# Two blocks in one kernel: row sums through DRAM, interleaved first stripes, a norm by token tile, and block 2's rows kept on chip

## The chip, the core and the metric

One core of a Trainium2 chip runs the whole program in one launch. Its engines are TensorE (PE, matmuls and transposes), VectorE (DVE), ScalarE (ACT), GpSimd (POOL) and SyncE (SP, which here only issues DMAs). The metric is the device time of one launch in microseconds. Three runs of the kernel before gave 2902.57, 2904.52 and 2905.27; the median is 2904.52.

## The reference, cut to what matters

Input is one sequence of 256 tokens of width 2048, all in float32. Two blocks follow each other.

```
block 1: shift, scale, gate = split(silu(c) @ w_ada + b_ada);  same for the context
  h  = rmsnorm(x) * (1 + scale) + shift;      p = h @ w_in            (9216 columns)
  hc = the same for 256 context tokens;       kc, vc = hc @ w_in[K, V]
  attention of 12 query heads over [k, kc];   fourier mix of u_b (fft over tokens and channels)
  y = (sig(g_a) * ((attn*silu(z_a)) @ w_proj_a) + sig(g_b) * ((mix*silu(z_b)) @ w_proj_b)) @ w_out
  x = rmsnorm(x + gate * y) * final_g
block 2: six modulation vectors = silu(c_2) @ w_mod + b_mod
  u = rmsnorm(x)*norm1*(1+scale1)+shift1;     proj = u @ w_in_2       (18464 columns)
  o_a = stick-breaking attention, 16 heads (sigmoids times running products)
  q, k, v = silu(causal conv of 4 taps);  g = -exp(a_log)*softplus(a_b + dt_bias);  beta = sig(b_b)
  o_b = gated delta rule, 16 heads:  gc = cumsum(g);  decay[r,i] = exp(gc[r]-gc[i]) for i <= r;
        a triangular system per 64 tokens (here solved per 128), a state carried over
  h = x + gate1 * ((sig(gate_a)*(o_a @ p_a) + sig(gate_b)*(o_b @ p_b)) @ w_out)
  u = rmsnorm(h)*norm2*(1+scale2)+shift2
  h = h + gate2 * ((silu(u @ w_gate) * (u @ w_up)) @ w_down)           (5632 wide)
```

## The kernel before

**Chunks and stripes.** All large products run as one stream. A stripe is 512 output columns for 256 tokens (two token tiles m of 128, one PSUM bank each); a chunk is 256 rows of a stripe's weights, 512 KB, as two 128x512 tiles. To keep float32's precision weights and activations are split in two parts each: ACT writes `w_hi` (L412), DVE writes `w_lo = raw - w_hi` (L422), and PE does x_hi*w_hi, x_lo*w_hi (L666) and x_hi*w_lo (L672), 12 matmuls per chunk. Activations stand transposed in `hT` or `fT`, each as hi and lo.

**Buffers.** SP loads raw chunks into six slots (L362), and there are three slots of split weights. At beat n (one beat per chunk) ACT and DVE split chunk n+3 once PE is done with chunk n; SP loads chunk n+6. Each engine is in order: whatever it waits for holds its next split.

**Modulation.** Eight stripes of block 1's modulation ("ada", 64 chunks) have only two tokens as operand: 4 matmuls per chunk (L652, L656), and one chunk per stripe is taken unsplit (`plain`, L642). ACT copies each row out (L868), PE turns it into columns (L876), and DVE and ACT prepare the first operands from it (L893, L903, L909). The other 28 x 8 modulation chunks are elementwise products with sums on DVE (L686), placed at fixed beats (`mod_at`).

**Order.** `of_chunk` is the order: three ada stripes, then a quarter (2 chunks each) of the first three ordinary stripes (two of the context, one of w_in), two ada stripes, a quarter, three ada stripes, two quarters; then phases in1, ab1 (the two projections, merged by gates), out1, in2 (starts at chunk B), pb2, ab2, out2, ffa (gate and up, starts at FFB), dna (down, first 12 chunks per stripe), ffb, dnb (down, the rest). Everything else is a side track: a list of (beat, steps), where `yield k` puts the following instructions at that beat after the start; a track is itself in order, so a later item waits for the end of an earlier one.

**Ends of stripes.** A "store" stripe is copied from PSUM by ACT and DVE and stored to DRAM. A "rows" stripe (out1, out2, dnb) is multiplied by the gate and added to the rows `E[:, 0:2]` by DVE (`add_rows`, L456, L459, L461, L463), and ACT sums squares (L474, L481). In dna the stripes are stored to DRAM, `h2` too, and `base_dve` (L1049, L1052) brings both back early in dnb.

**Norms.** Between out1 and in2, and between out2 and ffa, no product can run before the row norm. DVE reduces the sums (L488 to L498), POOL takes the power -1/2 (L502), DVE scales (L509), PE transposes (L524), ACT writes hi (L534) and b - hi (L540), DVE writes lo (L548). in2's first chunk waits for lo.

**Small projection and running sums.** `w_ba` (2048x32) is loaded at beat B+12 in pieces of 128 bytes (L1369), split by ACT and DVE (L1401, L1428) and multiplied (L1376, L1377). From its columns come the decays; for each of four turns (4 heads, GD_AT) PE makes gc along rows by 8 matmuls of a broadcast column with an upper triangle (L1574, "R"), read by DVE (L1763, L1767) and ACT from PSUM.

**Block 2's attention** (SB_AT, 8 turns of 2 heads; L1997, L2005, L2012, L2020 on PE) stands in one track with the turns of the delta rule and with the transposes of its output (L940) on PE, ACT and DVE.

**Merge gates.** In ab2 SP loads the gates at beat 3 of the first turn (L744), and ACT takes their sigmoid at its beat 1 (L757), waiting for the load.

Of the kernel before, what the change touches and what calls it, by code (L numbers as in the profile page):

```python
# [20 lines left out]
F32 = mybir.dt.float32  # L21
# [5 lines left out]
P = 128  # L27
D = 2048
# [109 lines left out]
def program(nc, a, y_out, dram):  # L138
    ctx = ExitStack()
    with ctx:  # L140
# [60 lines left out]
        ff_sig, ff_row, mg_tmp = E[:, 0, 0:M * W], E[:, 1, 0:M * W], E[:, 1, M * W:]  # L201
# [82 lines left out]
        for k in range(4):  # L284
            st = stripe("dna", 2 * FA, tile_of(a["w_down_2"], k * W), fT, 0, "store", cols_of(dram.ya, k * W))
# [3 lines left out]
        plan(S)  # L289

# [6 lines left out]
        of_chunk = whole(ADS[:3]) + quarter(0) + whole(ADS[3:5]) + quarter(1) + whole(ADS[5:]) + quarter(2) + quarter(3)  # L297
# [11 lines left out]
        ends = {st.end - 1: st for st in ADS + S}  # L309
        at_chunk = {}  # L310
# [60 lines left out]
        def store(sp, st):  # L371
            if st.kind == "store":
                sp.wait_ge(s["ev_act"], st.sn)
                sp.wait_ge(s["ev_dve"], st.sn)
                sp.dma_start(st.dst, ost[:, st.slot]).then_inc(s[f"stored{st.slot}"], 16)
            elif st.phase == "dnb":
# [65 lines left out]
        def add_rows(dve, st):  # L442

            cols = slice(st.o * W, (st.o + 1) * W)
            if st.o == 0:

                dve.wait_ge(s["gr_ld"], 16 * ((st.res - 1) // 4 + 1))
                if st.phase != "dnb":
# [5 lines left out]
            staging(dve, st)  # L454
            o = ost[:, st.slot]
            nc.vector.tensor_tensor(o, ps[:, st.bank:st.bank + M], bm(E[:, 3, cols], M), ALU.mult).then_inc(s["res_mul"], 1)  # L456
# [5 lines left out]
            else:  # L462
                nc.vector.tensor_tensor(E[:, 0:2, cols], E[:, 0:2, cols], o, ALU.add).then_inc(s["res"], 1)  # L463

        def square_rows(act, st):
# [10 lines left out]
            if st.phase != "dnb":  # L476
# [7 lines left out]
        def norm_stat_dve(dve, u):  # L484

            dve.wait_ge(s["sq"], (16, 24)[u])
            wait(dve, s["n_rs"], 2 * u)
            nc.vector.tensor_reduce(nms[:], nss[:].rearrange("p k m o -> p (k m) o"), AX.X, ALU.add).then_inc(s["n_v"], 1)  # L488
            dve.wait_ge(s["n_v"], 3 * u + 1)
            if u == 0:  # L490
                nc.vector.tensor_scalar(nms[:], nms[:], 1.0 / D, None, ALU.mult).then_inc(s["n_v"], 1)
                dve.wait_ge(s["n_v"], 2)
                nc.vector.tensor_scalar(nms[:, 0:M], nms[:, 0:M], EPS, None, ALU.add).then_inc(s["n_v"], 1)
                dve.wait_ge(s["n_v"], 3)
                nc.vector.scalar_tensor_tensor(nms[:, M:], nms[:, 0:M], EPS, nms[:, M:], ALU.mult, ALU.add).then_inc(
                    s["n_ms"], 1)
            else:
                nc.vector.tensor_scalar(nms[:, M:], nms[:, M:], 1.0 / D, EPS, ALU.mult, ALU.add).then_inc(s["n_ms"], 1)  # L498

        def norm_pool(pool, u):  # L500
            pool.wait_ge(s["n_ms"], u + 1)
            nc.gpsimd.tensor_tensor(nrs[:, M:], nms[:, M:], neghalf[:, 0:M], ALU.pow).then_inc(s["n_rs"], 1)  # L502
# [3 lines left out]
        def norm_scale_dve(dve, u, q):  # L506
            dve.wait_ge(s["n_rs"], 2 * u + 1)
            for m in range(M):
                ins = nc.vector.tensor_scalar(E[:, 2 + m, q * W:(q + 1) * W], E[:, m, q * W:(q + 1) * W],  # L509
                                              nrs[:, M + m:M + m + 1], None, ALU.mult)  # L510
            ins.then_inc(s["n_z"], 1)
# [4 lines left out]
        def norm_pe(pe, u, q):  # L516

            pe.wait_ge(s["n_z"], 4 * u + q + 1)
            if q >= 2:
                pe.wait_ge(s["n_lo"], KT * u + G4 * (q - 1))  # L520
            for j in range(G4):
                for m in range(M):
                    at = q * W + j * P
# [1864 lines left out]
```

## Time and profile before

| | |
|---|---|
| median of 3 runs | 2904.52 us |
| profiled execution, its own time | 2904.66 us |
| its span, first to last instruction | 2902.7 us |
| PE busy | 2833.5 us (98%) |
| DVE, ACT, POOL busy | 1962.1 (68%), 1348.4 (46%), 73.3 (3%) |
| mean granted TensorE clock | 0.991 of 2.4 GHz |
| chain that ended last | PE 89%, DVE 4%, DMA 2%, ACT 2%, issue 2%, POOL 1% |
| landing of a load, median | weights 512 KB 4.3 to 8.2 us; 1 MB loads 6.4 to 13.9 us; w_ba 256 KB 7.5 us |
| traffic | 711.81 MB, mean 245 GB/s |

Busy is the union of an engine's instructions; matmuls overlap in the records, so PE's pace is read from the starts of groups of four. The granted clock is a share of full speed: 1.00 is 2.4 GHz, and a stretch below it is part at 1.2 GHz. Times with a point in the text, such as 818.03, are microseconds from the span's start.

### The profile page before, as it was taken

The page shows a single profiled execution, that of the slowest core. Times are in us where ns is not written, and L with a number is a line of the kernel's source. Part 1 is how long each engine was busy: PE and PEld are TensorE (multiplying, and loading weights), DVE is VectorE, ACT ScalarE, POOL GpSimd, SP SyncE. Part 2 cuts the span into 40 slices and gives each one's busy share as a digit, 9 for nine tenths or more (in the row PEclk, how much of TensorE's full clock was granted, in tenths as well). Part 3 has the DMA queues.
Part 4 walks back from the last instruction along what each step waited for, and adds up shares of the span by engine and source line. Part 5 has one row for each costly group of instructions (what it writes and reads, how often), then busy time and mean ns, then how long its engine had stood idle before and what let it go on. Part 6 is the DMA issues. An engine that isn't in the chain of part 4 may idle for free.

```text
span 2902.7 us, 36566 instructions
## 1 busy us (share of the span) xinstructions
PE 2833.5 (98%) x13592; PEld 2311.0 (80%) x13592; DVE 1962.1 (68%) x2413; ACT 1348.4 (46%) x1726; POOL 73.3 (3%) x49
## 2 busy tenths in 40 slices
PE   7899999999989999999999999999999999999999
PEld 3478888878877888888888888887878888888877
DVE  6778777758866868677775787765657664445564
ACT  6545444444463535353534555544454444344433
POOL 0000000000000101010100000000000000000000
PEclk8999999999999999999999999999999999999999
DMA  8889777768958556556557788777657776665664
GB/s 313 313 325 343 265 243 253 272 231 333 352 207 308 182 204 196 197 175 213 185 190 243 258 304 303 285 258 257 237 188 280 268 249 195 203 196 191 203 244 145
DMA packets 223825, 711.81 MB, mean 245 GB/s; under 512 B 26816, under 2 KB 42528, under 8 KB 220576
## 3 DMA queue, kind: packets, MB, share of 16 engines
q1 hardware_dynamic: 222496, 705.17, 69.8%
q0 software_dynamic: 576, 4.19, 0.3%
q8 instruction: 108, 1.77, 0.2%
q14 instruction: 69, 0.57, 0.1%
q10 hardware_dynamic: 576, 0.11, 0.0%
HBM read 665.30 MB, written 44.09 MB: 244 GB/s over the span
## 4 chain that ended last, share of the span: by engine, by line
PE 89%; DVE 4%; DMA 2%; ACT 2%; issue 2%; POOL 1%; SPq 0%; DVEq 0%; ACTq 0%
PE ps L666 51%; PE ps L672 25%; PE ps L1597 1%; PE ps L1607 1%; DVE w_lo L422 1%; ACT w_hi L412 1%; PE ps L1261 1%; PE ps L1246 1%; PE ps L1601 1%; PE ps L792 1%; DVE mraw L686 1%; POOL arena L1824 1%; DMA E<-in_ctx 1%; DMA raw<-in_w_ada 0%; DMA raw<-in_w_in 0%
## 5 line engine op out<-in xcount | busy, mean ns | idle before, releaser
L412 ACT CAST w_hi<-raw 128x1024 fp32r<-128x1024 f32 x928 | 971.6, 1049 | 1436.8 <-PE ps L672 1390.5
L422 DVE TENSOR_TENSOR w_lo<-raw,w_hi 128x1024 fp32r<-128x1024 f32 x928 | 1128.7, 1223 | 604.9 <-ACT w_hi L412 603.5
L666 PE MATMUL ps<-w_hi,hT_hi 128*128 128x512 f32 x2688 | 745.8, 399 | 4.9 <-ACT w_hi L412 3.1
L666 PE MATMUL ps<-w_hi,hT_lo 128*128 128x512 f32 x2688 | 721.7, 390 | 0.0
L672 PE MATMUL ps<-w_lo,hT_hi 128*128 128x512 f32 x2688 | 719.6, 389 | 1.1 <-DVE w_lo L422 1.0
L666 PEld LDWEIGHTS ps<-w_hi,hT_lo 128*128 128x128 f32 x2688 | 505.6, 188 | 109.1
L672 PEld LDWEIGHTS ps<-w_lo,hT_hi 128*128 128x128 f32 x2688 | 504.7, 188 | 108.1 <-DVE w_lo L422 2.3
L666 PEld LDWEIGHTS ps<-w_hi,hT_hi 128*128 128x128 f32 x2688 | 491.0, 189 | 103.0 <-issue 10.1
L686 DVE SCALAR_TENSOR_TENSOR mraw<-mraw,sB 128x1024 f32<-128x1024 f32 x224 | 273.3, 1220 | 6.9 <-DMA mraw<-in_w_modt 6.9
L666 PE MATMUL ps<-w_hi,fT_hi 128*128 128x512 f32 x800 | 222.4, 400 | 0.5 <-ACT w_hi L412 0.5
L672 PE MATMUL ps<-w_lo,fT_hi 128*128 128x512 f32 x800 | 219.3, 396 | 1.9 <-DVE w_lo L422 1.9
L666 PE MATMUL ps<-w_hi,fT_lo 128*128 128x512 f32 x800 | 220.4, 397 | 0.0
L672 PEld LDWEIGHTS ps<-w_lo,fT_hi 128*128 128x128 f32 x800 | 150.4, 188 | 38.8 <-DVE w_lo L422 2.3
L666 PEld LDWEIGHTS ps<-w_hi,fT_lo 128*128 128x128 f32 x800 | 151.4, 189 | 36.8
L666 PEld LDWEIGHTS ps<-w_hi,fT_hi 128*128 128x128 f32 x800 | 149.6, 189 | 35.9 <-issue 1.1
L581 DVE COPY ost<-ps 128x512 f32<-128x512 f32 x64 | 44.1, 690 | 25.8 <-PE ps L672 20.4
L1724 DVE SCALAR_TENSOR_TENSOR arena<-ps,arena 128x255 f32<-128x255 f32 (+2 forms) x144 | 59.3, 477 | 0.2 <-ACT arena L1645 0.2
L1800 DVE TENSOR_TENSOR arena<-arena,ps 128x1024 f32<-128x1024 f32 x24 | 29.3, 1222 | 43.2 <-PE ps L1607 43.2
L656 PE MATMUL ps<-w_lo,sT 128*4 128x512 f32 x112 | 38.4, 427 | 13.2 <-DVE w_lo L422 12.4
L652 PE MATMUL ps<-w_hi,sT 128*4 128x512 f32 x112 | 38.7, 429 | 10.1 <-ACT w_hi L412 10.1
L1607 PEld LDWEIGHTS ps<-arena 128*128 128x128 f32 x384 | 46.6, 191 | 1.8
L1597 PEld LDWEIGHTS ps<-arena 128*128 128x128 f32 x384 | 46.6, 191 | 1.8
(301 smaller groups left out, 1737.2 us busy)
## 6 DMA issues: line engine op xcount, KB each, us to landing
raw<-in_w_in SPq DMA_DIRECT2D x432, 512.0 KB, 4.6
mraw<-in_w_modt SPq DMA_DIRECT2D x224, 512.0 KB, 4.4
raw<-in_w_gate SPq DMA_DIRECT2D x88, 512.0 KB, 4.3
raw<-in_w_up SPq DMA_DIRECT2D x88, 512.0 KB, 4.3
raw<-in_w_down SPq DMA_DIRECT2D x88, 512.0 KB, 4.3
raw<-in_w_ada SPq DMA_DIRECT2D x64, 512.0 KB, 5.6
raw<-in_w_out SPq DMA_DIRECT2D x64, 512.0 KB, 4.6
scratch_p<-ost SPq DMA_DIRECT2D x54, 512.0 KB, 5.8
```

Of the source, the lines that this page charges most:

```text
L412: nc.scalar.copy(w_hi[:, to], raw[:, slot]).then_inc(s["hi"], 1)
L422: nc.vector.tensor_tensor(w_lo[:, to], raw[:, slot], w_hi[:, to].bitcast(F32), ALU.subtract).then_inc(s["lo"], 1)
L581: evac(dve, st, 1, lambda dst, src: nc.vector.tensor_copy(dst, src), "ev_dve")
L652: pe.matmul(ada_out(st.idx), sT[:, kc * CK + t], w_hi[:, slot, t], start=(kc == 0 and t == 0), stop=False)
L656: mm = pe.matmul(ada_out(st.idx), sT[:, kc * CK + t], w_lo[:, slot, t], start=False, stop=(kc == st.chunks - 1 and t == CK - 1))
L666: pe.matmul(bank(st.bank + m), x, w_hi[:, slot, t], start=(kc == 0 and t == 0 and xp == 0), stop=False)
L672: mm = pe.matmul(bank(st.bank + m), x, w_lo[:, slot, t], start=False, stop=(kc == st.chunks - 1 and t == CK - 1))
L686: nc.vector.scalar_tensor_tensor(w, w, 1.0, sB[:, h], ALU.mult, ALU.mult, accum_out=macc[:, j % 2, mk // 2, mk % 2:mk % 2 + 1]).then_inc(s ...
L1597: mm = pe.matmul(tiles(4)[:, t], gL[:, t], gXT[:, t], start=True, stop=True)
L1607: mm = pe.matmul(tiles(4)[:, t], gX[:, t], gR[:, t], start=True, stop=True)
L1724: ins = vec.scalar_tensor_tensor(y, x, cw[:, k, h, 3 - j:4 - j], y, ALU.mult, ALU.add)
L1800: GV.done(vec.tensor_tensor(gXT, gXT, tiles(4), ALU.subtract), f"xt{lv}")
```

## The change

- `of_chunk`: after three ada stripes the remaining ada chunks alternate evenly with those of the quarters; four ordinary chunks and the last quarter follow.
- Last stripe of out1, out2 and dnb (`by_m`): its last two chunks run for token tile 0 first, then for tile 1 (`last_rows_pe`); rows are added, squared and stored by tile; ACT's and DVE's splits for the two chunks after the stripe move behind that.
- Norm statistics, scaling and transposes by tile; the first stripe's x_hi products wait for hi alone.
- `w_ba` comes laid out by partition, is loaded at OUT1+12 and split at OUT1+25.
- The running sums are transposed once, stored to DRAM, and broadcast to all partitions by two DMAs per turn.
- Block 2's attention has a track of its own; its last two steps come a beat later.
- The merge's sigmoid in ab2 comes at beat 3; each gate buffer has its own semaphore.
- dna's stripes are added to the rows; `base_dve`, the stores of `ya` and `h2` and their reloads go; gate 2 is loaded in two halves beside the temporaries of the feed-forward part, which move. The residual rows' loads are spread over beats 5 and 7.

```diff
-        of_chunk = whole(ADS[:3]) + quarter(0) + whole(ADS[3:5]) + quarter(1) + whole(ADS[5:]) + quarter(2) + quarter(3)
+        def woven(a, b):
+            both = [((i + 0.5) / len(a), 0, c) for i, c in enumerate(a)] + [((i + 0.5) / len(b), 1, c) for i, c in enumerate(b)]
+            return [c for _, _, c in sorted(both, key=lambda item: item[:2])]
+        of_chunk = whole(ADS[:3]) + woven(whole(ADS[3:5]), quarter(0)) + woven(whole(ADS[5:7]), quarter(1))
+        of_chunk += woven(whole(ADS[7:]), quarter(2)[:2]) + quarter(2)[2:] + quarter(3)
...
+            st.by_m = st.phase in ("out1", "out2", "dnb") and st.o == 3
...
-            st = stripe("dna", 2 * FA, tile_of(a["w_down_2"], k * W), fT, 0, "store", cols_of(dram.ya, k * W))
+            st = stripe("dna", 2 * FA, tile_of(a["w_down_2"], k * W), fT, 0, "rows")
...
+        def add_rows_m(dve, st, m):
...
+            if m == 0:
+                dve.wait_ge(s["half"], st.half)
...
+            o, e = ost[:, st.slot, m], E[:, m, cols]
+            nc.vector.tensor_tensor(o, bank(st.bank + m), gate_part(st), ALU.mult).then_inc(mul, 1)
+            dve.wait_ge(mul, done)
+            if st.phase == "out1":
+                nc.vector.tensor_tensor(o, o, e, ALU.add).then_inc(x, 1)
+                dve.wait_ge(x, done)
+                nc.vector.tensor_tensor(e, o, E[:, 2, cols], ALU.mult).then_inc(res, 1)
+            else:
+                nc.vector.tensor_tensor(e, e, o, ALU.add).then_inc(res, 1)
...
+        def last_rows_pe(pe, st):
+            pe.wait_ge(s["lo"], halved[st.end])
+            for m in range(M):
+                for kc in (st.chunks - 2, st.chunks - 1):
+                    slot = halved[st.end - st.chunks + kc] % HL
+                    for xp, wp in ((0, w_hi), (1, w_hi), (0, w_lo)):
+                        for t in range(CK):
+                            x = st.buf[xp][:, st.k0 + kc * CK + t, m * P:(m + 1) * P]
+                            mm = pe.matmul(bank(st.bank + m), x, wp[:, slot, t], start=False,
+                                           stop=(kc == st.chunks - 1 and t == CK - 1 and wp is w_lo))
+                if m == 0:
+                    mm.then_inc(s["half"], 1)
+            mm.then_inc(s["pe"], 2)
...
             if st.phase in ("in2", "ffa") and st.o == 0:
-                pe.wait_ge(s["n_lo"], KT * (st.phase == "ffa") + CK * (kc + 1))
+                pe.wait_ge(s["n_hi"], KT * (st.phase == "ffa") + CK * (kc + 1))
...
+                    if xp == 1 and st.phase in ("in2", "ffa") and st.o == 0:
+                        pe.wait_ge(s["n_lo"], KT * (st.phase == "ffa") + CK * (kc + 1))
...
             def norm_x1(dve):
-                norm_stat_dve(dve, 0)
-                for q in range(4):
-                    norm_scale_dve(dve, 0, q)
-                for q in range(2):
-                    norm_lo_dve(dve, 0, q)
+                for m in range(M):
+                    norm_stat_dve(dve, 0, m)
+                for m in range(M):
+                    for q in range(2):
+                        norm_scale_dve(dve, 0, q, m)
+                split_lo(dve, B + 1)
+                norm_lo_dve(dve, 0, 0)
+                for q in (2, 3):
+                    for m in range(M):
+                        norm_scale_dve(dve, 0, q, m)
+                norm_lo_dve(dve, 0, 1)
+                split_lo(dve, B + 2)
...
         def merge_sig_act(act, st):
-            yield 1
-            act.wait_ge(s["mg_ld"], 32 * (st.mg + 1))
+            yield 3 if st.kind == "mp" else 1
+            act.wait_ge(s[f"mg_ld{st.mg % 2}"], 32 * (st.mg // 2 + 1))
...
-            load_rows(sp, f"resid{k}", 0)
-            load_rows(sp, f"resid{k}", 1)
+            for m in range(M):
+                yield 2 + 2 * m
+                load_rows(sp, f"resid{k}", m)
...
-            sp.dma_start(braw, a["w_ba"].rearrange("(t p) n -> p t n", p=P)).then_inc(s["ba_ld"], 16)
+            sp.dma_start(braw, a["w_ba"]).then_inc(s["ba_ld"], 16)
...
+            pe.transpose(bank(5)[0:NB, 0:P], gcol(GC), c.ident[:]).then_inc(s["ba_pe"], 1)
...
+        def gc_sp(sp, i):
+            yield 0
+            sp.wait_ge(s["gc_act"], 1)
+            sp.dma_start(dram.glog, gc_rows).then_inc(s["gc_st"], 16)
+        def gdn_r_sp(sp, i):
+            yield 0
+            sp.wait_ge(s["gc_st"], 16)
+            if i > 0:
+                GV.after(sp, i - 1, "os")
+            for m in range(M):
+                row = dram.glog[m * NH2 + i * GB:m * NH2 + (i + 1) * GB].rearrange("(o h) p -> o (h p)", o=1)
+                sp.dma_start(gR[:, m * GB:(m + 1) * GB].rearrange("p h t -> p (h t)"), row.to_broadcast([P, GB * P])).then_inc(
+                    s["gd_r"], 16)
...
-            for t in range(GT):
-                mm = pe.matmul(tiles(4)[:, t], gb[:, LOGG, t:t + 1].to_broadcast([P, P]), c.upper[:], start=True,
-                               stop=True)
-            GP.done(mm, "R")
...
-            GP.after(dve, i, "R")
+            dve.wait_ge(s["gd_r"], 32 * (i + 1))
...
-            items += [(OUT1 + 3, resid_sp, 1), (B + 12, ba_sp, 0)]
+            items += [(OUT1 + 3, resid_sp, 1), (OUT1 + 12, ba_sp, 0)]
+            items += [(B + 26, gc_sp, 0)] + [(GD_AT[i] + 8, gdn_r_sp, i) for i in range(NH2 // GB)]
...
-            stream_pe(pe, [first, [(14, silu_row_pe, 0)], adas, gates, items, turns], {B: norm_x1, FFB: norm_h2})
+            stream_pe(pe, [first, [(14, silu_row_pe, 0)], adas, gates, items, sorted(sbs, key=lambda item: item[0]), turns], {B: norm_x1, FFB: norm_h2})
```

## Rows read from the trace of the kernel before

**Rows 1.** PE's waits by line and releaser: total, times, longest.
```profile
PE ps L524 <- DVE E L509: 14.3, 2, 8.2
PE ps L656 <- DVE w_lo L422: 12.4, 12, 1.7
```

**Rows 2.** Timeline from 1945: start, duration, engine, line, operation; idle before and releaser.
```profile
1968.03 1.07 PE L666 MATMUL ps<-w_hi,hT_hi 128*128 128x512 f32 x4
...
1970.75 1.07 PE L666 MATMUL ps<-w_hi,hT_hi 128*128 128x512 f32 x4
...
1973.80 1.91 ACT L757 ACTIVATE E<-E 128x2048 f32<-128x2048 f32 x1 [5.88 <-DMA E<-scratch_p]
...
1981.20 1.08 PE L666 MATMUL ps<-w_hi,hT_hi 128*128 128x512 f32 x4
```

**Rows 3.** Timeline of the early dnb phase.
```profile
2811.92 1.09 PE L666 MATMUL ps<-w_hi,fT_hi 128*128 128x512 f32 x4
...
2812.25 2.29 DVE L1052 TENSOR_TENSOR E<-E 128x2048 f32<-128x2048 f32 x1 [2.77 <-DMA E<-scratch_h]
...
2821.22 1.09 PE L666 MATMUL ps<-w_hi,fT_hi 128*128 128x512 f32 x4
...
2824.02 1.09 PE L666 MATMUL ps<-w_hi,fT_hi 128*128 128x512 f32 x4
```

**Rows 4.** PE's timeline in the modulation's chunks.
```profile
84.79 0.63 PE L652 MATMUL ps<-w_hi,sT 128*4 128x512 f32 x2
...
85.72 0.63 PE L652 MATMUL ps<-w_hi,sT 128*4 128x512 f32 x2
```

**Rows 5.** Groups by line, 59.55 to 191: count, busy, mean ns, idle before.
```profile
L422 DVE TENSOR_TENSOR w_lo<-raw,w_hi 128x1024 fp32r<-128x1024 f32 x61 | 73.2, 1224 | 32.5 <-ACT w_hi L412 32.2
```

**Rows 6.** Stretches: length, busy PE, PEld, DVE, ACT, POOL; clock, DMA share, GB/s.
```profile
78.67:103.04 24.37, 20.45 (x74) 5.83 (x72) 19.84 (x27) 15.68 (x18) 0.00 (x0) 0.93 0.92 308
103.04:121.57 18.53, 18.06 (x81) 14.23 (x80) 9.34 (x9) 7.72 (x8) 0.00 (x0) 1.00 1.00 388
121.57:156.39 34.82, 28.99 (x113) 8.73 (x112) 28.20 (x36) 23.63 (x27) 0.00 (x0) 1.00 0.89 302
```

**Rows 7.** Timeline between out1 and in2, the first norm.
```profile
818.03 1.23 DVE L456 TENSOR_TENSOR ost<-ps,E 128x1024 f32<-128x1024 f32 x1 [0.36 <-PE ps L672]
...
824.48 0.70 POOL L502 TENSOR_TENSOR nrs<-nms,neghalf 128x2 f32<-128x2 f32 x1 [313.23 <-DVE nms L495]
...
828.16 1.02 ACT L534 ACTIVATE hT_hi<-ps,modv,A 128x256 fp32r<-128x256 f32 x2 [4.56 <-PE ps L524]
...
830.59 1.16 PE L666 MATMUL ps<-w_hi,hT_hi 128*128 128x512 f32 x4 [0.76 <-issue]
```

**Rows 8.** Timeline between out2 and ffa, the second norm.
```profile
2145.46 1.23 DVE L456 TENSOR_TENSOR ost<-ps,E 128x1024 f32<-128x1024 f32 x1 [0.43 <-PE ps L672]
...
2156.04 1.17 PE L666 MATMUL ps<-w_hi,hT_hi 128*128 128x512 f32 x4 [0.96 <-issue]
```

**Rows 9.** Timeline around the small projection.
```profile
872.06 0.60 SPq L1369 DMA_DIRECT2D arena<-in_w_ba  x1
...
880.96 0.33 PE L1377 MATMUL ps<-hT_hi,b_two 128*64 128x256 f32 x1 [4.03 <-DVE b_two L1428]
...
886.17 0.28 PE L1377 MATMUL ps<-hT_hi,b_two 128*64 128x256 f32 x1
886.29 1.09 PE L666 MATMUL ps<-w_hi,hT_hi 128*128 128x512 f32 x4
```

**Rows 10.** Timeline of the first turn's running sums, one of four.
```profile
994.81 1.95 PE L1574 MATMUL ps<-c_upper,arena 128*128 128x128 f32 x16
...
996.51 1.17 PE L666 MATMUL ps<-w_hi,hT_hi 128*128 128x512 f32 x4
```

**Rows 11.** Timeline of block 2's first attention turn.
```profile
1614.99 1.58 PE L1997 MATMUL ps<-c_ident,arena 128*128 128x128 f32 x8 [2.22 <-DVE arena L1935]
...
1620.29 1.50 PE L2005 MATMUL ps<-arena 128*128 128x128 f32 x12
```

More of the change, by code:

```diff
@@ L70, in __init__ @@
         self.kind, self.dst = kind, dst
+        self.by_m, self.half = False, 0
 class Track:
@@ L289, in program @@
         plan(S)
+        for st in S:
+            st.by_m = st.phase in ("out1", "out2", "dnb") and st.o == 3
+            st.half = ("out1", "out2", "dnb").index(st.phase) + 1 if st.by_m else 0
         def whole(stripes):
@@ L309, in program @@
         ends = {st.end - 1: st for st in ADS + S}
+        joint = {st.end - 2 + k for st in S if st.by_m for k in range(2)}
         at_chunk = {}
@@ L375, in store @@
                 sp.dma_start(st.dst, ost[:, st.slot]).then_inc(s[f"stored{st.slot}"], 16)
+            elif st.by_m and st.phase == "dnb":
+                for m in range(M):
+                    sp.wait_ge(s["res"] if m else s["res_h"], st.res if m else st.half)
+                    sp.dma_start(rows(y_out[0], m)[:, st.o * W:(st.o + 1) * W], E[:, m, st.o * W:(st.o + 1) * W]).then_inc(
+                        s["out_st"], 16)
             elif st.phase == "dnb":
@@ L555, in stream_act @@
             for beat in range(CHUNKS):
-                if beat + HL < CHUNKS:
+                if beat + HL < CHUNKS and beat not in joint:
                     split_hi(act, beat + HL)
@@ L561, in stream_act @@
                         evac(act, st, 0, lambda dst, src: nc.scalar.copy(dst, src), "ev_act")
+                    elif st.kind == "rows" and st.by_m:
+                        if st.phase != "dnb":
+                            for m in range(M):
+                                square_rows_m(act, st, m)
+                            split_hi(act, st.end + 1)
+                            split_hi(act, st.end + 2)
                     elif st.kind == "rows":
@@ L581, in stream_dve @@
                         evac(dve, st, 1, lambda dst, src: nc.vector.tensor_copy(dst, src), "ev_dve")
+                    elif st.kind == "rows" and st.by_m:
+                        for m in range(M):
+                            add_rows_m(dve, st, m)
                     elif st.kind == "rows":
@@ L589, in stream_dve @@
                     side.run(beat)
-                if beat + HL < CHUNKS:
+                if beat + HL < CHUNKS and beat not in joint:
                     split_lo(dve, beat + HL)
@@ L661, in stream_pe @@
                     continue
+                if st.by_m and kc >= st.chunks - 2:
+                    if kc == st.chunks - 1:
+                        last_rows_pe(pe, st)
+                        for side in sides:
+                            side.run(n)
+                    continue
                 for xp in range(2):
+                    if xp == 1 and st.phase in ("in2", "ffa") and st.o == 0:
+                        pe.wait_ge(s["n_lo"], KT * (st.phase == "ffa") + CK * (kc + 1))
                     for t in range(CK):
@@ L1686, in gdn_act @@
             GV.after(act, i, "dt")
-            GA.done(A_.activation(g_eg, tiles(4)[:, GB:GT], ACT.Exp), "eg")
+            act.wait_ge(s["gd_r"], 32 * (i + 1))
+            GA.done(A_.activation(g_eg, gR[:, GB:GT], ACT.Exp), "eg")
             GA.done(A_.activation(gDT, gDT, ACT.Exp), "edt")
@@ L2105, in _ @@
             norm_pool(pool, 1)
-            pool.wait_ge(s["res"], 8)
-            for m in range(M):
-                pool.dma_start(rows(dram.h2, m), E[:, m]).then_inc(s["r_st"], 16)
         @block.scalar
```

279 lines of the change are left out of this document (159 added, 120 removed).

## The prediction

> **What bounds the kernel now.** I read the page's busy shares first: TensorE (PE) is busy for 98% of the span and the next engine for 68%, and the chain of waits goes through PE for 89%. So an edit counts only where it takes work off PE or closes a gap or slow spot of PE. PE's waits come next [rows 1]: the longest kind is the wait for the rows of the two norms, then the wait for a split-off low part (w_lo). All its gaps together are 2902.7 - 2833.5 = 69 us; the rest of the possible gain is work removed, and work done at the lower clock. The timeline then gives the unit in which I count: a chunk is 12 matmuls, 2.72 us with hT as operand (1968.03 to 1970.75, [rows 2]) and 2.80 with fT (2821.22 to 2824.02, [rows 3]); a modulation chunk is 4 thin matmuls, 0.93 us [rows 4]; its plain form takes 1.88. DVE needs 1.22 us to split any chunk [rows 5], so it can't feed modulation chunks at PE's pace but has 1.5 us to spare beside an ordinary one.
>
> **The change part by part** (gain against the profiled execution).
>
> *1. First stripes' chunks alternate with the modulation's.* From 59.55 to 190.90 us PE has 24 ordinary chunks (66.6 us), 40 modulation chunks of which 5 plain (35 x 0.93 + 5 x 1.88 = 42) and 6 groups of small products of about 1 us: 114 to 115 us of work in 131.4, so 17 us are lost, nearly all in the first and last stretch of [rows 6]: 16 modulation chunks in a row in 24.37 us (work about 18) and 24 in 34.82 (work about 28). There DVE is 81% busy while PE waits. Interleaved, a group of one ordinary and 2.67 modulation chunks costs PE 2.8 + 2.5 = 5.3 us, DVE 3.67 x 1.22 = 4.5, and loads 1.92 MB, 364 GB/s, below the 388 that the DMA reached in an ordinary block (second row of [rows 6]). PE becomes the limit. Not all comes back: only three split buffers exist, so after an ordinary chunk the third thin one is still ready some 0.3 us late; and the constants, 17 DMAs queued by SP (SyncE) at the same beat, still hold weight loads up for 8 us, some 2 us of which I leave standing. I take 11.5. Bounds: 17 above; below 5, if only the chunks next to an ordinary one gain. A loss has its own place among the rivals.
>
> *2. Norm by token tile, last two chunks by token tile.* At the first norm PE's last chunk is done when DVE starts at 818.03; the next chunk starts at 830.59 [rows 7]: 12.6 us. In it: three DVE operations of 1.23, then to POOL's start at 824.48 the last squares (1.6) and four tiny statistics (0.8, with signals 1.1), POOL's 0.70, scaling, transposes up to the high parts at 828.16 (2 in 1.02), their differences and the low parts. Afterwards tile 0's half of the last stripe is finished 2.72 us early and its rows are done before PE ends. From PE's end only tile 1 is on the path: three half-size operations 2.0, last square with its read 0.85, statistics 0.8, POOL 0.7 and its signal, one scale 0.5, four transposes 0.6, high parts 1.05 and signals 0.2: 6.7 us. The first chunk now waits for the high part alone, and its second four matmuls for the low part, some 0.4 more. Gain 12.6 - 7.1 = 5.5. At the second norm 2145.46 to 2156.04 = 10.6 us [rows 8] has one operation and one square fewer per tile: after, 0.65 less in operations and 0.4 less in statistics, 6.0; gain 4.6. Queued behind: the splits of the next two chunks move behind the squares on ACT (ScalarE) and between the scales on DVE; the third chunk's low part comes about 14.5 us after PE's end where PE wants it at 15.3. Together 10.1. Bounds: 7 (both those splits late) and 11.5 (no wait for the low part).
>
> *3. Small projection (w_ba) loaded in one piece per partition and split long before.* PE waited 4.03 us for the split and then ran the products slowly, since it had idled: from 880.96 - 4.03 to the next chunk at 886.29 [rows 9] 9.4 us; 32 products at 0.12, the pace of the last one, are 3.7. Gain 5.8; at least the wait, 4.0. The load was issued at 872.06, nine microseconds before; now it goes out 20 chunks before the phase's end and has over 50 us.
>
> *4. Running sums through DRAM.* Each of four turns loses 16 passes on PE: 994.81 to 996.51 [rows 10] = 1.70, together 6.8. One transpose comes in, 0.27 at most: 6.5. The two broadcasts per turn are issued at beat 8 by SP, which stands some 2.5 chunks ahead of PE, and wanted by DVE at beat 17: over 25 us, where the slowest 1 MB load of the page took 13.9 and these are 0.25 MB. ACT's copy and SP's store happen once; SP may wait a beat for that copy, with six chunks loaded ahead. So nothing on the path. DVE and ACT read SBUF in place of PSUM, off the path. Bounds 6 and 7.5.
>
> *5. Block 2's attention in a track of its own, two of its steps a beat later.* Its first turn had to queue behind the transposes of the linear part: PE waited 2.22, and eight transposes and a chunk after it ran slowly, 1614.99 to 1620.29 [rows 11] = 5.3 for 1.0 + 2.72: 3.8 us in all, which go since the turn starts two beats earlier. The later steps take in waits of 1.1 (for the weights of attention) and 1.2 (for their copy) of the same list as [rows 1], of which I take 1.8. Sum 5.6; bounds 2.2 and 6.1.
>
> *6. Sigmoid of the merge's first gates two beats later on ACT.* ACT stood for the load until 1973.80 with the splits of three chunks behind it; PE took 1970.75 to 1981.20 for two chunks [rows 2]: 10.45 - 5.44 = 5.0 lost. Two beats are 5.4 us, ACT then reaches the sigmoid at about 1972, waits 2 us, and PE's next split is done at 1978 where it is wanted at 1980.7. I take 4.6; at least the 3.1 that PE stood idle.
>
> *7. Block 2's rows stay on chip.* Four DVE operations of 2.28 us and two reloads go; two of them stood in front of a low part, and PE took 2811.92 to 2821.22 for two chunks [rows 3], 9.30 - 5.60 = 3.7. The stores they replace were no PE time. The down phase's first half now ends each stripe with two DVE operations of 1.23 in place of one copy on each engine; the second half has the same today and holds 2.80 per chunk. Gain 3.7, lower bound 1.9 (the idle alone). The late row loads (two and four beats after the gate's row) are issued some 5 us before DVE wants them; today's burst also lands 1.5 us after it is wanted, without cost to PE, so 0.
>
> *8. End.* The two DVE operations after the last matmul halve (2.45 to 1.3), the last store is half as big: 1.3 (0.5 to 2).
>
> Sum: 11.5 + 10.1 + 5.8 + 6.5 + 5.6 + 4.6 + 3.7 + 1.3 = 49.1. The profiled execution took 2904.66 us (span 2902.7), 0.1 over the median of the runs, so the two need no correction: 2904.66 - 49.1 = 2855.6. All lower bounds together give 29.7 (2875), all upper ones 59 (2846).
>
> **Rivals.**
> A. *The weave gives little*: after an ordinary chunk the splits of the thin ones come late each time, so that three buffers set the pace and not the mean load. Worked out: 0.5 us in each of 14 groups, 2 us for the constants, and the last preparation late by 2: 11 of 17 remain, gain 6; with the norms at their lower bound too, 2855.6 + 5.5 + 3.1 = 2864. For it: the long runs show DVE-set gaps of 1.25. Against: beside an ordinary chunk DVE idles 1.5 us now.
> B. *More than counted*: PE never falls to the lower clock in the woven part and the constants' hold is covered: 17 and 11.5, giving 2855.6 - 5.5 - 1.4 = 2849.
> C. *Slower: the woven part runs at half clock.* Mechanism: an ordinary chunk between thin, partly idle ones no longer finds 2.4 GHz. In the first row of [rows 6] the granted clock is 0.93 and after a wait a chunk with its transposes took 5.3 for 3.7 [rows 11], so stretches at 1.2 GHz exist. The woven part holds 14 ordinary and 40 modulation chunks with their products, about 87 us; at half clock it takes 87 more, less the 17 of stalls, while the rest gives 37.6: 2904.66 + 70 - 37.6 = 2937. It decides once over 55 us of that work run at 1.2 GHz. Against it: in the last row of [rows 6], with PE idle for 5.8 of 34.8 us, the granted clock was 1.00.
> The Trainium skill, "TensorE: Matmul & The Clock Gate", section "HAM oscillation — how this bites in real kernels", tells of layouts whose thin computing between waits lets the clock drop again at every step. By that rule the woven part would be nearer to C, 2937; the trace agrees at the gaps of several microseconds, and not for the short gaps of the thin runs, so C's chance stays small.
> D. *It does not do what it says at the norms*: tile 0 is not early, since DVE reaches it late, or the low part of the third chunk holds PE: gain 4 of 10, 2862.
>
> **How the numbers follow.** Forecast with its own band 2850 to 2861: 0.58. A 0.15, B 0.12, D 0.10, C 0.02, and 0.03 for a mixture that leaves 2870 to 2899. Range 2847 to 2868. A change under 0.2% (5.8 us) can't be told from none here. Faster 0.97, same 0.01, slower 0.02.
>
> **What would show it.** In the changed kernel's trace: the first ordinary block (stripe 4) starts near 179.5 in place of 190.9; from the last matmul of the output projection to the next chunk 7 us in place of 12.6, and 6 in place of 10.6; no wait for b_two, none for the merge's gate and none in the down phase; no passes with c_upper as moving side in the turns; the granted clock near 1.00 throughout after 60 us. It would be wrong if PE's waits for w_lo grew in the front, if DVE waited for the broadcast rows, or if PE's gaps came back at the second and third chunk after each norm.

## The result and the profile after

The changed kernel took 2874.28 us (median; 2873.23 to 2875.66) beside 2904.89 for the kernel before on the same chip: 0.989 of it, 95% interval 0.9876 to 0.9903. The forecast was a gain of 49.1 us, to 2855.6; it gained 30.6, and the time lies outside the range. The profiled execution took 2873.23 us with a span of 2870.7, 32.0 less than before; the two profiled executions differ by 31.4. The accounts below are of the spans.

First the page's busy times and PE's share of the chain, then PE's longest waits, in the changed kernel:

```profile
PE 2819.8 (98%) x13529; PEld 2300.9 (80%) x13529; DVE 1968.4 (69%) x2426; ACT 1346.5 (47%) x1723; POOL 78.7 (3%) x49
...
PE 91%; DVE 4%; DMA 2%; issue 1%; ACT 1%; POOL 1%; SPq 0%; DVEq 0%; ACTq 0%
```
```profile
PE ps L749 <- ACT w_hi L442: 10.4, 4, 7.3
PE ps L753 <- DVE w_lo L452: 7.8, 8, 1.7
PE ps L596 <- DVE E L583: 7.3, 2, 4.3
PE ps L777 <- DVE w_lo L452: 7.2, 3, 6.4
PE ps L771 <- ACT w_hi L442: 3.9, 1, 3.9
```

PE still sets the time. The wait of the norms' transposes has halved, 14.3 to 7.3 [rows 1]; the wait for w_lo in the modulation's chunks fell from 12.4 to 7.8, of which 6.7 and 6.6 lie in the first 60 us, ahead of the woven part: there it fell from 5.7 to 1.2. Two waits are new: one of 6.4 us at L777, an ordinary chunk, and one of 3.9 at L771. These two lead to what went wrong.

The gain is read by laying the two traces chunk by chunk beside each other: the start of the same chunk before, minus its start after, is what has been won up to there.

| Chunk | before | after | won so far | in this stretch | forecast |
|---|---|---|---|---|---|
| first ordinary block (stripe 4) | 190.90 | 187.12 | 3.8 | 3.8 (step 1) | 11.5 |
| 12 chunks into the output projection | 763.43 | 768.02 | -4.6 | -8.4 (row loads, in step 7) | 0 |
| second chunk after the first norm | 833.43 | 833.51 | -0.1 | 4.5 (step 2) | 5.5 |
| behind the small projection | 886.29 | 880.30 | 6.0 | 6.1 (step 3) | 5.8 |
| behind the fourth turn's transposes | 1450.85 | 1437.86 | 13.0 | 7.0 (step 4) | 6.5 |
| start of the second merge phase | 1958.94 | 1940.45 | 18.5 | 5.5 (step 5) | 5.6 |
| second output projection | 2054.79 | 2031.28 | 23.5 | 5.0 (step 6) | 4.6 |
| second chunk after the second norm | 2158.86 | 2132.16 | 26.7 | 3.2 (step 2) | 4.6 |
| 13 chunks into the last phase | 2821.22 | 2790.82 | 30.4 | 3.7 (step 7) | 3.7 |
| end of span | 2902.7 | 2870.7 | 32.0 | 1.6 (step 8) | 1.3 |

Six terms came within 0.5 us. Step 1 fell 7.7 short, one clause of step 7 cost 8.4 where it said 0, and step 2 is 2.4 short: 18.5 less, and 1.4 more in the other steps: 49.1 - 17.1 = 32.0.

**The new wait of 6.4.** The timeline of the output projection in the changed kernel (start, duration, engine, line, operation; in brackets the idle time before and what ended it):

```profile
737.88 0.36 SPq L1151 DMA_DIRECT2D E<-scratch_gr  x1
...
739.51 0.42 SPq L1092 DMA_DIRECT2D E<-in_x  x1
...
744.73 0.43 SPq L1092 DMA_DIRECT2D E<-in_x  x1
...
757.66 1.22 DVE L488 TENSOR_TENSOR ost<-ps,E 128x1024 f32<-128x1024 f32 x1 [9.04 <-DMA E<-in_x]
...
762.59 2.07 PE L777 MATMUL ps<-w_lo,hT_hi 128*128 128x512 f32 x4 [6.40 <-DVE w_lo L452]
...
764.46 1.91 PE L771 MATMUL ps<-w_hi,hT_hi 128*128 128x512 f32 x4
```

and the same place in the kernel before:

```profile
742.06 1.11 SPq L988 DMA_DIRECT2D E<-in_x  x2
...
753.91 1.22 DVE L456 TENSOR_TENSOR ost<-ps,E 128x1024 f32<-128x1024 f32 x1 [1.51 <-DMA E<-in_x]
```

The second row load left SP at 744.73 and DVE started at 757.66, 12.9 us later; before, the second of the two left at 742.54 (it is inside the row that starts at 742.06) and DVE started 11.4 us later. In the changed kernel DVE stood 9.04 us with the low parts of the next weights behind it, and PE, which had no split weights left, stood 6.40 and then ran two groups of four matmuls in 2.07 and 1.91 us in place of 1.07.

**The new wait of 3.9.** SP's queue and the first split behind it:

```profile
89.77 0.42 SPq L2165 DMA_DIRECT2D c_upper<-in_c_upper  x1
...
97.85 0.43 SPq L2165 DMA_DIRECT2D c_dt_bias<-in_c_dt_bias  x1
98.33 0.43 SPq L387 DMA_DIRECT2D raw<-in_w_kv  x1
...
101.99 1.04 ACT L442 CAST w_hi<-raw 128x1024 fp32r<-128x1024 f32 x1 [6.16 <-DMA raw<-in_w_kv]
...
103.18 1.30 PE L771 MATMUL ps<-w_hi,fT_hi 128*128 128x512 f32 x4 [3.92 <-ACT w_hi L442]
```

SP issues 17 constants from 89.77 to 98.28, half a microsecond each, and no weight load in between. The stretches of [rows 6] in the changed kernel (length, busy time of PE, PEld, DVE, ACT and POOL, granted clock, DMA share, GB/s):

```profile
78.67:103.04 24.37, 19.94 (x83) 10.23 (x81) 16.95 (x24) 13.52 (x16) 0.00 (x0) 1.00 0.93 326
103.04:121.57 18.53, 18.39 (x72) 10.88 (x73) 12.35 (x11) 10.36 (x11) 0.00 (x0) 0.91 0.98 382
121.57:156.39 34.82, 33.91 (x142) 17.83 (x140) 27.07 (x35) 22.12 (x26) 0.00 (x0) 1.00 0.87 319
```

The weave works where nothing disturbs it: in the last stretch PE is busy for 33.9 of 34.8 us (28.99 before). In the first it is idle 4.4 us, and the clock is lower just behind that.

### The profile page after: what moved, and what is told of

Its sections match the earlier page's. It is cut to its first block, busy times and chain, and to the rows that moved or that the text cites. A ratio compares the mean times of both kernels' runs of the same rounds, so it can differ in the third digit from the quotient of the medians.

```text
span 2870.7 us, 36454 instructions
## 1 busy us (share of the span) xinstructions
PE 2819.8 (98%) x13529; PEld 2300.9 (80%) x13529; DVE 1968.4 (69%) x2426; ACT 1346.5 (47%) x1723; POOL 78.7 (3%) x49
## 4 chain that ended last, share of the span: by engine, by line
PE 91%; DVE 4%; DMA 2%; issue 1%; ACT 1%; POOL 1%; SPq 0%; DVEq 0%; ACTq 0%
PE ps L771 52%; PE ps L777 26%; PE ps L1715 1%; PE ps L1705 1%; DVE w_lo L452 1%; DMA mraw<-in_w_modt 1%; PE ps L1347 1%; PE ps L1332 1%; PE ps L753 1%; PE ps L1709 1%; PE ps L718 1%; PE ps L897 1%; PE ps L749 1%; DVE mraw L791 1%; POOL arena L1936 1%
## 5 line engine op out<-in xcount | busy, mean ns | idle before, releaser
L771 PE MATMUL ps<-w_hi,hT_hi 128*128 128x512 f32 x2680 | 743.7, 399 | 0.8 <-issue 0.8
L777 PE MATMUL ps<-w_lo,hT_hi 128*128 128x512 f32 x2680 | 718.3, 390 | 7.2 <-DVE w_lo L452 7.2
L771 PE MATMUL ps<-w_hi,hT_lo 128*128 128x512 f32 x2680 | 718.5, 390 | 0.1
L777 PEld LDWEIGHTS ps<-w_lo,hT_hi 128*128 128x128 f32 x2680 | 503.0, 188 | 114.9 <-DVE w_lo L452 9.7
L771 PEld LDWEIGHTS ps<-w_hi,hT_lo 128*128 128x128 f32 x2680 | 503.1, 188 | 109.0 <-DVE hT_lo L621 0.5
L771 PEld LDWEIGHTS ps<-w_hi,hT_hi 128*128 128x128 f32 x2680 | 489.5, 189 | 99.0 <-issue 7.7
L771 PE MATMUL ps<-w_hi,fT_hi 128*128 128x512 f32 x784 | 217.4, 399 | 5.5 <-ACT w_hi L442 3.9
L771 PE MATMUL ps<-w_hi,fT_lo 128*128 128x512 f32 x784 | 215.5, 396 | 0.0
L777 PE MATMUL ps<-w_lo,fT_hi 128*128 128x512 f32 x784 | 215.4, 396 | 0.0
L771 PEld LDWEIGHTS ps<-w_hi,fT_hi 128*128 128x128 f32 x784 | 146.3, 189 | 41.4 <-issue 4.7
L771 PEld LDWEIGHTS ps<-w_hi,fT_lo 128*128 128x128 f32 x784 | 147.9, 189 | 36.0
L777 PEld LDWEIGHTS ps<-w_lo,fT_hi 128*128 128x128 f32 x784 | 147.8, 189 | 35.9
L1705 PE MATMUL ps<-arena 128*128 128x128 f32 x384 | 46.7, 275 | 0.0
```

Source lines behind the costliest of these rows:

```text
L771: pe.matmul(bank(st.bank + m), x, w_hi[:, slot, t], start=(kc == 0 and t == 0 and xp == 0), stop=False)
L777: mm = pe.matmul(bank(st.bank + m), x, w_lo[:, slot, t], start=False, stop=(kc == st.chunks - 1 and t == CK - 1))
L1705: mm = pe.matmul(tiles(4)[:, t], gL[:, t], gXT[:, t], start=True, stop=True)
```

## The experiments

Each was timed in five rounds beside the kernel before, four kernels on one chip at a time (2905.97, 2905.53 and 2906.66 us for the kernel before in the three groups). The ratio is to that. There is no run 5. Two kernels that differ by less than some 7 us have overlapping intervals; there single times and the traces are read too. The start of the first ordinary block in executions with the same front varies by 2 us (187.12 in the changed kernel, 188.13 in its second timing, 186.02 in run 1).

| Run | median us | ratio | 95% interval | span |
|---|---|---|---|---|
| changed kernel, run again | 2875.04 | 0.9893 | 0.9879 to 0.9906 | 2871.5 |
| 1 rows together | 2865.23 | 0.9857 | 0.9843 to 0.9870 | 2861.9 |
| 2 constants spread | 2868.24 | 0.9868 | 0.9855 to 0.9882 | 2868.5 |
| 3 chunks in runs again | 2877.02 | 0.9898 | 0.9883 to 0.9913 | 2875.0 |
| 4 before, rows late | 2914.63 | 1.0029 | 1.0018 to 1.0039 | 2912.7 |
| 6 chunks in runs, constants spread | 2878.26 | 0.9905 | 0.9892 to 0.9919 | 2874.0 |
| 7 rows and constants | 2859.19 | 0.9841 | 0.9827 to 0.9854 | 2857.2 |
| 8 and modulation later | 2857.99 | 0.9835 | 0.9821 to 0.9848 | 2855.5 |
| 9 constants from GpSimd | 2871.55 | 0.9882 | 0.9868 to 0.9895 | 2868.6 |
| 10 before, weave, spread | 2896.82 | 0.9968 | 0.9957 to 0.9980 | 2897.6 |
| 11 sigmoid early | 2861.98 | 0.9849 | 0.9835 to 0.9862 | 2861.3 |
| 12 attention steps back | 2860.84 | 0.9845 | 0.9831 to 0.9858 | 2858.2 |

The changed kernel run again, beside runs 6 to 8:

> The changed kernel itself, on the chip and in the hour of the runs beside it, as the zero of their comparisons: 2872 to 2877.

It took 2875.04 us, 0.8 from its first timing and inside the expected 2872 to 2877.

**The rows, from both sides (1 and 4).** Run 1 takes the late row loads out of the changed kernel:

```
             for m in range(M):
-                yield 2 + 2 * m
                 load_rows(sp, f"resid{k}", m)
```

> The changed kernel with one edit: the rows that the residual adds need are issued together again, right behind the gate's row, instead of two and four beats after it. Theory R (the late row loads were costed at nothing and cost 8.4 us in the first output projection): the loss at the first output projection goes, 2874.3 - 8.4 = 2865.9, within 2864 to 2868, and DVE waits under 3 us for the rows where it now waits 9.04. Rival Q (the rows are late because the whole DMA stream is behind at that place, whenever they are issued): under 2 us of gain, 2872 to 2875, and PE's wait for w_lo at that place stays.

Run 4 puts them into the kernel before:

```
-            load_rows(sp, f"resid{k}", 0)
-            load_rows(sp, f"resid{k}", 1)
+            for m in range(M):
+                yield 2 + 2 * m
+                load_rows(sp, f"resid{k}", m)
```

> The kernel before with one edit: the rows of the residual adds issued two and four beats after the gate's row, as in the changed kernel. Theory R (the shift alone costs, with DMA as full there as in the changed kernel): 7 to 9 us slower, 2912 to 2914. Rival Q (the loss needs the changed kernel's other traffic at that place): under 2 us, 2903 to 2907.

Measured: 9.0 us less, and 8.7 us more than before (2905.97 beside it). The time of run 4, 2914.63, is 0.6 above its range, since the kernel before was slower by 1.1 beside it; the difference is inside the 7 to 9 of theory R. R holds on both sides, and Q falls. The rows in run 1's trace, then in run 4's:

```profile
737.17 1.08 SPq L1092 DMA_DIRECT2D E<-in_x  x2
749.88 1.23 DVE L488 TENSOR_TENSOR ost<-ps,E 128x1024 f32<-128x1024 f32 x1 [2.38 <-DMA E<-in_x]
```
```profile
744.24 0.42 SPq L988 DMA_DIRECT2D E<-in_x  x1
749.46 0.42 SPq L988 DMA_DIRECT2D E<-in_x  x1
763.69 1.23 DVE L456 TENSOR_TENSOR ost<-ps,E 128x1024 f32<-128x1024 f32 x1 [10.34 <-DMA E<-in_x]
```

DVE's wait is 9.04 us with the delay and 2.38 without it in the changed kernel, 10.34 with and 1.51 without in the kernel before: in each pair this is the only edit. Run 1's 2.38 costs PE 0.5: the split buffers carry it.

**The constants and the weave (2, 3, 6, 9, 10).** Run 2, in the changed kernel:

```
-                for name, _ in dram.consts:
-                    if name not in EARLY + ("c_cols",):
-                        sp.dma_start(consts[name][:], ...)
+                sp.dma_start(consts[LATE[i]][:], ...)
-            items += ... [(40, consts_sp, 0)]
+            items += ... [(32 + i, consts_sp, i) for i in range(len(LATE))]
```

> The changed kernel with one edit: the 17 loads of constants, which SP issues in a row at beat 40, are issued one a beat from beat 32 on. Theory K (SP stands behind 17 issues of half a microsecond, the weight loads come out late, and PE waits 3.92 + 1.71 + small ones for the split of the weights, whatever the order of the chunks): 4 to 6 us of gain, 2868.3 to 2870.3. Rival L (the bytes of the constants are what hold the weights up, so that spreading them only spreads the loss): under 1.5 us, 2873 to 2875.

Run 3 puts the order of chunks back:

```
-        of_chunk = whole(ADS[:3]) + woven(whole(ADS[3:5]), quarter(0)) + ...
+        of_chunk = whole(ADS[:3]) + quarter(0) + whole(ADS[3:5]) + quarter(1) + whole(ADS[5:]) + quarter(2) + quarter(3)
```

> The changed kernel with one edit: the chunks of the first stripes go back into runs between the modulation's, as in the kernel before. Theory W (the weave is worth the 3.8 us by which the end of the front is earlier in the two traces): 2878.1, within 2877 to 2879.5. Rival V (the weave is worth the forecast 11.5, and something else of the change spoils the front by 7.7): 2884 to 2887. Rival N (worth nothing, the 3.8 comes from elsewhere): 2873 to 2875.

Run 6 has both edits:

> The changed kernel with two edits: chunks of the first stripes in runs again, and the constants' loads spread one a beat. With the constants spread the weave is worth 2868.2 against this. Theory I (constants' hold and thin runs are separate losses that add up; the weave is worth about 3 to 4 with or without the hold): 2871 to 2872.5. Rival H (the hold masks the weave's worth: DMA that stands behind the constants eats what the weave wins, and without the hold the weave gives 7 or more): 2875 or more, so that spreading gains nothing in runs.

Measured: spreading gains 6.0 us in the woven order (K), and the four times of run 2, 2866.69 to 2870.45, lie below all eight of the changed kernel (2871.87 to 2875.66). In the order of runs it gains none, 2877.0 to 2878.3 (H). By the medians the weave is worth 2.7 us with the burst of constants (2877.0 against 2874.3, W) and 10.0 without it (2878.3 against 2868.2). By the start of the first ordinary block it is 5.4 and 8.1: 192.56 to 187.12 with the burst, 192.03 to 183.89 with the loads spread. So the weave and the burst are coupled, in the direction of H, and the size of the coupling stays between 3 and 7 us. One thing beside the edits is mixed in: the kernel before, with the order and the burst of run 3, starts that block at 190.90, and from 125 to 150 us its granted clock was 1.00 where runs 3 and 6 show 0.87 and 0.86. Why the clock fell there in these two is open, and part of the 5.4 and 8.1 may be this. I take from run 6 that in runs the spread loads fall among the thin chunks, of which each 0.5 MB buys only 0.93 us of PE, and delay those instead; that reading was only argued.

Run 9 leaves the burst where it is and takes it off SP:

```
+            pool.wait_ge(s["pe"], 40)
+            for name, _ in dram.consts:
+                if name not in EARLY + ("c_cols",):
+                    pool.dma_start(consts[name][:], a["c_" + name]).then_inc(s["consts"], 16)
```

> The changed kernel with one edit: the same 17 loads of constants, still all at once and at the same place (when PE has done 40 chunks), but issued by GpSimd, which has nothing to do there, and not by SP. Theory K (SP's 17 issues in a row keep the weight loads from being issued): SP is free, so the gain is that of the spread loads, 2867 to 2870. Rival L (1.7 MB of constants at once hold up the weights' bytes, whoever issues them): 2872 to 2875, as the changed kernel.

Between the two theories: 2.7 us less than the changed kernel and 3.3 more than run 2 by the medians, with overlapping intervals; the first ordinary block starts at 184.90, between 187.12 and 183.89. PE's and ACT's waits from 90 to 190 and from 85 to 115 us, first in the changed kernel and then in run 9:

```profile
PE ps L771 <- ACT w_hi L442: 3.9, 1, 3.9
PE ps L771 <- DVE fT_lo L1014: 1.5, 1, 1.5
...
ACT w_hi L442 <- DMA raw<-in_w_kv: 6.2, 1, 6.2
```
```profile
PE ps L753 <- DVE w_lo L452: 1.7, 3, 0.6
PE ps L771 <- DVE fT_lo L1014: 1.5, 1, 1.5
PE ps L771 <- ACT w_hi L442: 1.1, 1, 1.1
...
ACT w_hi L442 <- DMA raw<-in_w_ada: 7.0, 6, 2.6
```

One wait of 6.2 for a load that was not issued has become six shorter ones, 7.0 in all, for loads that travel among the constants. So both theories seem to hold in part: SP's standing is one loss, the bytes at once the other. The Trainium skill, "DMA: Bandwidth & Descriptors", section "Issuing engines are not separate DMA queues", says that transfers issued by different engines share the same DMA engines and that another issuer saves only issue time; run 9 agrees as far as its size can be told: issue time is saved, and short waits among the bytes remain.

Run 10 puts the two edits alone into the kernel before:

> The kernel before with two edits alone: the weave of the first stripes' chunks, and the constants' loads one a beat. Theory H (the weave's forecast 11.5 holds once SP does not stand behind the constants): 9 to 11 us less than before, 2894.5 to 2896.5. Rival J (it was worth that only together with the rest of the change): 3 to 6 less, 2899 to 2902.

9.8 us less (2906.66 to 2896.82), and 8.7 of it by the start of the first ordinary block, 190.90 to 182.19. So the two edits need nothing else of the change. The profiled execution, the slowest of the six, gained only 5.1 over its span: at the two norms, which the edits do not touch, it gave back 2.2 and 2.4 (its granted clock over the 15 us of each was 0.54 and 0.56, and 0.66 and 0.77 in the kernel before).

**Both mended, and the last preparation (7 and 8).** Run 7 joins the edits of 1 and 2:

> The changed kernel with the rows issued together again and the constants' loads spread one a beat. Both losses apart: 2865.2 for the rows, 6.0 less for the constants, 2859 to 2861. Rival (they overlap, since the later part of the program takes back what the front wins): 2863 to 2866.

The two gains add, to 2859.19: 6.0 us below run 1, as run 2 is below the changed kernel. Run 8 adds:

```
-        mod_from = [... ((14, 2), (30, 2), ...
+        mod_from = [... ((17, 2), (30, 2), ...
```

> The kernel before this one in the list with a third edit: the first row of the second modulation's stream starts three beats later, out of the way of the last preparation, whose low part PE waits for by 1.5 us. Theory P: 1.2 to 1.7 us less than the run before it in the list, 2858. Rival (the wait only moves to the modulation's next row): no difference.

The time moved by 1.2 us, too little to tell from none; the trace does show the mechanism. PE's wait for fT_lo, 1.5 us in the changed kernel, is

```profile
PE ps L771 <- DVE fT_lo L1014: 0.4, 1, 0.4
```

in run 8, and the first ordinary block starts at

```profile
181.16 1.07 PE L771 MATMUL ps<-w_hi,hT_hi 128*128 128x512 f32 x4
```

against 181.92 in run 7. The first two stretches of [rows 6] in run 8:

```profile
78.67:103.04 24.37, 23.72 (x104) 13.52 (x102) 20.84 (x28) 17.12 (x20) 0.00 (x0) 1.00 1.03 393
103.04:121.57 18.53, 17.89 (x76) 9.85 (x74) 12.38 (x11) 10.59 (x12) 0.00 (x0) 1.00 1.02 393
```

PE is busy for 23.7 of 24.4 us where it was 19.9 in the changed kernel, at a granted clock of 1.00 and with 393 GB/s, above the 388 of the forecast. Run 8 is the fastest here: 47.5 us below the kernel before, 16 below the changed one.

**Two parts undone (11 and 12).** Run 11 is run 8 with `yield 3 if st.kind == "mp" else 1` back at `yield 1`; run 12 is run 8 with the transposes, copy and products of the attention's weights one beat earlier.

> The kernel with rows together, constants spread and the modulation's first row later (2858.0), with one part of the change undone: the sigmoid of the merge's first gates is issued two beats earlier again. Theory S (step 6, 4.6 forecast, 5.0 in the traces): 4 to 5.5 slower, 2862 to 2863.5. Rival (PE gets those microseconds from elsewhere since the loads come earlier now): under 2, 2858 to 2860.

> The same kernel (2858.0) with a part of step 5 undone: the transposes of block 2's attention weights and the products with them stand one beat earlier again, as before, on all three engines. Theory T (step 5 took 1.8 for these waits of 1.1 and 1.2): 1.5 to 2.5 slower, 2859.5 to 2860.5. Rival (the waits are covered by the split's slack either way): under 1 us.

4.0 and 2.9 us slower than run 8 by the medians, with overlapping intervals; run 12 lies 0.3 above the range of theory T. Chunk by chunk, the second merge phase alone loses 3.9 in run 11 and the attention alone 2.1 in run 12, which is inside T's; the rest of each difference lies where nothing was edited. Run 11's timeline:

```profile
1941.11 1.92 ACT L862 ACTIVATE E<-E 128x2048 f32<-128x2048 f32 x1 [4.74 <-DMA E<-scratch_p]
...
1944.10 1.16 PE L771 MATMUL ps<-w_hi,hT_hi 128*128 128x512 f32 x4 [2.08 <-ACT w_hi L442]
```

ACT stands for the load again, with the splits behind it. In the changed kernel the same operation has no wait:

```profile
1954.88 1.92 ACT L862 ACTIVATE E<-E 128x2048 f32<-128x2048 f32 x1
```

## Why the prediction was wrong, step by step

*The step that failed worst* is the last clause of step 7: "The late row loads (two and four beats after the gate's row) are issued some 5 us before DVE wants them; ... so 0". It judged a 1 MB load by when it is issued (3.9 us before DVE wanted it, as it turned out) and not by when it lands. The trace of before already gave the journey: the second load left at 742.54 and DVE went on at 753.91, 11.4 us later and 1.5 too late. The prediction's own step 4 goes by such a journey, the 13.9 us of the slowest 1 MB load. Against the chunks, the changed kernel issues the row load 6.0 us later (744.73 + 3.78 won so far - 742.54), and it took 1.6 us longer: 1.51 + 5.97 + 1.56 = 9.04, which is DVE's wait. The split buffers covered 2.6 of it (PE stood 6.40), and two groups at 2.07 and 1.91 us in place of 1.07 make up nearly all of the rest of the -8.4; runs 1 and 4 say -9.0 and -8.7 by the medians, and -7.6 and -10.2 at this place of their traces. The first two terms, 7.5, could have been had from the trace of before.

*Step 1*: the mechanism was right, its condition and its size were not. The condition: it gave the constants "some 2 us of which I leave standing". The same hold was there before, where it fell into a stretch that already waited. Once the weave had made PE the limit, more of it came through: spreading gained 6.0 by the medians in two pairs of kernels, 3.2 and 4.1 at the first ordinary block and 2.2 and 4.7 over the profiled spans, so that a part of the 6.0 is in no trace. The size: with these 2 us given back, the prediction's own sum would be 13.5, and the front ends only 8.7 (run 10) and 9.7 (run 8) earlier. In run 8 PE idles 2.6 us in all from its first ordinary chunk (62.06) to 181.16, at a granted clock of 1.00. So some 12 us, 9.7 + 2.6, were there to be won, and not 17; this is an estimate from run 8's trace. The trace of before said so too: PE idled 10.2 of the 131.4 us, at a granted clock of 0.98, and the two stretches that were to hold nearly all of the 17 hold 6.4 + 6.8 = 13.2 by the prediction's own figures. Its sum of work, 114 to 115 us, was too small: in run 8 PE is busy for 116.5 between those two points, with a first modulation chunk of the woven part already done.

The chance for a time between 2870 and 2899 was 0.03, and the time fell there. It also lies near the 2875 of all lower bounds together, which is chance: six of the terms were at their values and not at their bounds.

Rival A gave 2864 through splits that are late in each of 14 groups. In the last stretch of the woven part PE idles 0.9 of 34.8 us, and from 60 us on it waits for w_lo twice, 0.6 each, so this mechanism did not occur; that step 1 gave even less than A's 6 has the two causes above. Rival C, half clock in the woven part, is refuted: the granted clock was 1.00, 0.91 and 1.00 in the three stretches, and 0.92 from 59.5 to 80 us (0.93 before). The Trainium skill's rule that the prediction set beside C ("TensorE: Matmul & The Clock Gate", "HAM oscillation — how this bites in real kernels") tells of waits between thin computing, and the trace does not contradict it: the one long wait, 3.92, was followed by the 0.91, and the short gaps of the third stretch by 1.00.

*Step 2* is a size: 7.7 of 10.1. The second norm in the changed kernel:

```profile
2119.88 0.69 DVE L517 TENSOR_TENSOR E<-E,ost 128x512 f32<-128x512 f32 x1
...
2121.95 0.69 DVE L510 TENSOR_TENSOR ost<-ps,E 128x512 f32<-128x512 f32 x1 [1.38 <-PE ps L718]
2122.68 0.69 DVE L517 TENSOR_TENSOR E<-E,ost 128x512 f32<-128x512 f32 x1
2123.29 0.15 DVE L559 TENSOR_REDUCE nms<-nss 128x2 f32<-128x8 f32 x1
...
2124.42 1.83 DVE L583 TENSOR_SCALAR E<-E,nrs 128x512 f32<-128x512 f32 x4
2124.59 0.75 POOL L576 TENSOR_TENSOR nrs<-nms,neghalf 128x1 f32<-128x1 f32 x1 [0.32 <-DVE nms L571]
2124.95 3.51 PE L596 MATMUL ps<-c_ident,E 128*128 128x128 f32 x16 [3.04 <-DVE E L583]
...
2127.82 1.02 ACT L607 ACTIVATE hT_hi<-ps,modv,A 128x256 fp32r<-128x256 f32 x2 [1.81 <-PE ps L596]
...
2128.93 1.16 PE L771 MATMUL ps<-w_hi,hT_hi 128*128 128x512 f32 x4 [0.47 <-issue]
```

The forecast had 6.7 and 5.6 us from PE's last matmul to the next chunk, and 0.4 more for the low part that this chunk waits for. Measured are 7.5 at the first norm (822.73 to 830.26) and 7.0 at the second (2121.95 to 2128.93); the 0.4 came as forecast, at the second chunk (3.2 us behind the first in place of 2.8). Tile 0's rows are done before PE ends (2120.57), as forecast, but its statistics stand on DVE's queue behind tile 1's two operations and come at 2123.29. So its eight first transposes stand on PE just ahead of tile 1's four. PE has idled 3.04 us and does them at 0.22 apiece (3.51 for 16), where the forecast had 0.15: it leaves tile 0 at 2126.7, though tile 1's first scale is done at 2125.85. That is 0.9 of the 1.3 us at the second norm; tile 1's four transposes at the same slow pace are most of the rest. At the first norm the 0.8 is not taken apart. Rival D had said that DVE would reach tile 0 late; it did, at a smaller price than D's 6 us. No run tested this part alone; it rests on the traces.

*Steps 3, 4, 5, 6, 8 and the rest of 7* held within 0.5 us each. Step 3: the 32 products take 3.70 us at the full clock and no wait stands before them (876.60 to 880.30). Step 4: four times 1.6 to 1.8, no wait for the broadcast rows. Step 5: 2.8 at the first turn and 1.2 behind it, and 1.5 over the later ones (run 12 puts those at 2.1). Step 6: 5.0 (3.9 in run 11). All of these were single gaps of PE with both ends in rows.

## What to carry over

A load that is moved has to be costed by the time at which it lands, not the time at which it is issued: look up the same load's journey in the trace under the same traffic, add the shift, and hold it against the consumer's slack. Where an edit makes an engine the limit, list every hold in that stretch which the old waits covered, because each can come through afterwards; a burst of loads on the queue that feeds the limit is the first to look for. Hold a loss that is worked out as length minus work against the idle time that the trace shows: here 17 stood against 10.2. The single gaps of PE with both ends in rows came within half a microsecond here; the long covered stretch and the path through several engines at the norms did not.

## What the runs showed of the hardware

- The second 1 MB row load took 11.4 us from issue to use in the kernel before, 12.2 in run 1, 12.9 in the changed kernel (13.5 in its second timing) and 14.2 in run 4. It took longer where it was issued later behind the gate's row: eight earlier loads were then still under way, where five were in the kernel before and in run 1.
- Seventeen issues by SP in a row took 8.5 us (89.77 to 98.28), 0.5 each. Their loads add up to 2.1 MB in the trace's DMA view (1.7 in the expectations above), 5.5 us at the 382 GB/s of that neighbourhood (an estimate). The same issues on GpSimd's queue took 9.4 us.
- At the first norm of the changed kernel PE waited 4.26 us and then did 16 transposes in 3.01 us:

```profile
826.95 3.01 PE L596 MATMUL ps<-c_ident,E 128*128 128x128 f32 x16 [4.26 <-DVE E L583]
```

The first seven of them start about 0.11 us apart and the others 0.21. After 3.04 us at the second norm all 16 are about 0.21 apart, in 3.51 us, and in the second timing of the same kernel, with the same two waits, the 16 took 3.44 and 3.50. So the length of a wait alone did not set how soon the slower pace came.
